# A decoder step with experts: router products on h, grouped routing steps and norm sums on VectorE

## The reference, cut to what matters

```python
h = h + mixer_block(rmsnorm(h, g_mix), ...)        # convolution heads and SSD heads
h = h + hier_moe(rmsnorm(h, g_ffn), ...)
h = h + (p @ w_ple) * sigmoid(rmsnorm(h, g_ple) @ w_ple_gate)
y = rmsnorm(h, g_final)
# rmsnorm(x, g) = x * rsqrt(mean(x * x) + 1e-6) * g
# hier_moe, per row t: softmax over 4 groups, take the best group;
#   of its 4 experts take the best two; out = sum of weight * expert(t)
#   expert(t) = (silu(t @ w_gate_e) * (t @ w_up_e)) @ w_down_e
```

## Time and profile before

| what | value |
|---|---|
| median of three runs | 634.99 us (632.8 to 636.8) |
| the profiled execution | 639.18 us, its span 637.5 us |
| busy: TensorE, VectorE, ScalarE, GpSimd | 584.7, 265.0, 165.3, 81.3 us |
| the chain that ended last | TensorE 71%, DMA 14%, VectorE 5%, ScalarE 4% |
| out projection, second half, ends | 313.9 us |
| expert loop | 349 to 587 us |
| granted TensorE clock, mean | 0.955 of 2.4 GHz |

### The profile page before, as it was taken

How to read it: one execution, slowest core, us unless ns; L and a number is a source line. 1 busy time by engine, 2 the same in 40 slices (tenths; PEclk the granted TensorE clock), 3 DMA queues, 4 the chain that set the end, 5 groups by cost and what they waited for, 6 DMA issues and landing times.

```text
span 637.5 us, 8072 instructions
## 1 busy us (share of the span) xinstructions
PE 584.7 (92%) x2961; PEld 384.5 (60%) x2961; DVE 265.0 (42%) x797; ACT 165.3 (26%) x376; POOL 81.3 (13%) x90
## 2 busy tenths in 40 slices
PE   4999999999889987999877999999999999999993
PEld 3688888868677775888645343434343434434782
DVE  1699888503384786101155023224040404132333
ACT  3211311142457686321213010101101110103313
POOL 4000056023124430020000000000000000000000
PEclk9899999999779998999978989899999999998998
DMA  9643344378415542277941799999999999997001
GB/s 338 197 156 133 137 162 165 114 50 230 156 67 148 190 135 91 76 265 301 422 189 59 282 401 416 420 417 425 421 421 421 424 421 421 422 421 325 0 1 68
DMA packets 30171, 157.86 MB, mean 248 GB/s; under 512 B 6168, under 2 KB 8520, under 8 KB 13760
## 3 DMA queue, kind: packets, MB, share of 16 engines
q1 hardware_dynamic: 24960, 139.69, 55.8%
q0 software_dynamic: 4864, 17.54, 9.2%
q10 hardware_dynamic: 320, 0.27, 0.1%
HBM read 147.13 MB, written 8.21 MB: 244 GB/s over the span
## 4 chain that ended last, share of the span: by engine, by line
PE 71%; DMA 14%; DVE 5%; ACT 4%; issue 2%; SPq 1%; POOLq 0%; DVEq 0%; ACTq 0%
PE ps L796 18%; DMA xbc<-u_rows,slot_tok 11%; PE ps L1059 9%; PE ps L931 9%; PE ps L1030 9%; PE ps L1085 5%; PE ps L1073 4%; PE ps L763 2%; PE ps L846 2%; DMA ring<-glu 2%; PE ps L989 2%; PE ps L787 2%; SPq L347 1%; PE ps L983 1%; PE ps L811 1%
## 5 line engine op out<-in xcount | busy, mean ns | idle before, releaser
L796 PE MATMUL ps<-u,ring 128*128 128x264 f32 x640 | 144.1, 387 | 0.0
L796 PEld LDWEIGHTS ps<-u,ring 128*128 128x128 f32 x640 | 121.0, 190 | 21.1 <-issue 0.4
L1030 PE MATMUL ps<-ring,xraw 128*64 128x512 f32 x512 | 114.7, 601 | 1.2 <-ACT xraw L714 1.2
L1030 PEld LDWEIGHTS ps<-ring,xraw 128*64 128x64 f32 x512 | 35.7, 138 | 68.9 <-issue 68.8
L1503 DVE TENSOR_TENSOR h<-h,ps 128x264 f32<-128x264 f32 x64 | 27.5, 429 | 87.6 <-PE ps L1073 86.7
L931 PE MATMUL ps<-cat,ring 128*128 128x264 f32 x256 | 59.9, 394 | 2.8 <-DVE cat L1352 2.8
L1059 PE MATMUL ps<-ring,xraw 128*64 128x512 f32 x256 | 59.7, 620 | 0.0
L931 PEld LDWEIGHTS ps<-cat,ring 128*128 128x128 f32 x256 | 49.7, 195 | 12.0 <-issue 3.2
L507 POOL DMA_INDIRECT xbc<-u_rows,slot_tok x9 | 8.5, 948 | 285.6 <-DVE slot_tok L1469 285.6
L1059 PEld LDWEIGHTS ps<-ring,xraw 128*64 128x64 f32 x256 | 18.3, 144 | 36.2 <-issue 36.2
L464 POOL TENSOR_TENSOR glu<-asg 128x256 f32<-128x256 f32 x8 | 21.4, 2670 | 99.4 <-ACT asg L578 99.4
(11 more groups left out here) (252 smaller groups left out, 664.8 us busy)
## 6 DMA issues: line engine op xcount, KB each, us to landing
ring<-in_w_moe SPq DMA_DIRECT2D x96, 1024.0 KB, 14.0
ring<-in_w_in SPq DMA_DIRECT2D x20, 1024.0 KB, 5.0
ring<-in_w_out SPq DMA_DIRECT2D x8, 1024.0 KB, 4.9
ring<-in_state_s POOLq DMA_DIRECT2D x8, 512.0 KB, 9.5
out_h_s_out<-ring POOLq DMA_DIRECT2D x8, 512.0 KB, 5.6
ring<-in_w_pleg SPq DMA_DIRECT2D x4, 1024.0 KB, 20.0
ring<-glu SPq DMA_DIRECT2D x48, 32.9 KB, 2.6
h<-in_xT SPq DMA_DIRECT2D x2, 528.0 KB, 4.7
```

The source lines that it names most:

```text
L796: ins = mm(ps[:, BANK[n], 0:T], wv[:, k, q * P:(q + 1) * P], u[:, k, :], start=(k == 0), stop=(k == KD - 1))
L1030: ins = mm(ps[e * CAP:(e + 1) * CAP, gu, :], xg[:, 4 * hf + k, e * CAP:(e + 1) * CAP], wv[:, k, :], start=(hf == 0 and k == 0), stop=(hf = ...
```

## The change

- `load_table(Ln)` loads a table set that holds Ln and Exp, in place of a call of Ln.
- Norm 2: u is h x gain without the root, made by ScalarE behind each square. VectorE adds up the squares of seven blocks; TensorE adds the last and takes the mean (`mean_of_sum`).
- The router's weights are multiplied by the gain on GpSimd, and its products run on h itself: four blocks at a time, each into its own 32 partitions of a PSUM bank (`raw_logits`). VectorE multiplies the result by the root; a product with `fold` adds the four groups and turns to token order. Biases are added there.
- Token rows get the root when ScalarE copies them out (`keep_rows`), which needs the root in token order (`rs_tok`).
- Group and experts are chosen in one pass over five sets of four (the groups and each group's experts). The slots' base is a product with `iota16`; places and totals are two separate waits. The weights of the rows are worked out behind the slot list.
- The p product is split: blocks 0 and 1 ahead of the place products, 2 and 3 ahead of the slot products, 4 to 7 behind.
- Gate: ScalarE makes u as h is added; VectorE squares and adds up for norm 3. Norm 4: VectorE adds up squares between blocks, ScalarE makes `yo` = h x gain, and VectorE multiplies by the root two blocks at a time.
- `fold` gets a tile of its own, and three loads at the start share a semaphore.

```diff
             def load_table(func):
+                if func == ACT.Ln:
+                    a.preload_act_table_set("natural_log_exp_and_others")
+                    return
                 a.activation(warm[:, n_warm[0]:n_warm[0] + 1], eps[:, 0:1], func)
...
                 square(2, c, sq2)
-            root(2)
+                a.activation(u[:, c, :], h[:, c, :], ACT.Copy, scale=par("g_ffn", c)).then_inc(u_ready, 1)
+            root(2, rs_ffn)
+            act.wait_ge(logt_psum, 2)
+            a.activation(rs_tok[:, 0:2], ps[:, 0, 300:302], ACT.Copy)
+            link(a.activation(rs_tok[0:NSM, 2:3], ps[0:NSM, 0, 302:303], ACT.Copy))
+            def keep_rows(t):
+                tn = TOK[t][1]
+                act.wait_ge(utok_psum, t + 1)
+                a.activation(utok[0:tn, t, :].rearrange("p (b n) -> p b n", b=2), ps[0:tn, 2 + 2 * t:4 + 2 * t, :],
+                             ACT.Copy, scale=rs_tok[0:tn, t:t + 1]).then_inc(utok_ready, 1)
+            keep_rows(0)
+            keep_rows(1)
...
-                square(3, c, cat)
+                a.activation(u[:, c, :], h[:, c, :], ACT.Copy, scale=par("g_ple", c)).then_inc(u_ready, 1)
...
+            def mean_of_sum(i, x, last, between=None):
+                bank = NORM_BANK[i]
+                pe.wait_ge(sq_sum, i - 1)
+                ins = mm(ps[:, bank, 0:T], mean_k[:, :], x[:, 0, :], start=True, stop=not last)
+                if between:
+                    between()
+                for c in last:
+                    pe.wait_ge(sq_ready, KD * (i - 1) + c + 1 - (KD if i == 4 else 0))
+                    ins = mm(ps[:, bank, 0:T], mean_k[:, :], x[:, c, :], start=False, stop=(c == last[-1]))
+                ins.then_inc(stat_ready, 1)
...
-            for n in range(KD + 2):
-                if n < KD:
-                    w_out_half(n, 1).then_inc(o_psum, 1)
-                if n >= 2:
-                    mean_square(2, sq2, n - 2)
...
+            def raw_logits(half):
+                pe.wait_ge(o_added, 4 * half + 4)
+                for b in range(4):
+                    c = 4 * half + b
+                    ins = mm(ps[32 * b:32 * b + 32, 1, 0:T], wr[:, c, :], h[:, c, :], start=(half == 0), stop=(half == 1))
+                return ins
+            for n in range(KD):
+                w_out_half(n, 1).then_inc(o_psum, 1)
+                if n == 5:
+                    pe.wait_ge(wr_ready, 1)
+                    raw_logits(0)
+            mean_of_sum(2, sq2, [KD - 1], lambda: raw_logits(1).then_inc(log_psum, 1))
...
+            pe.wait_ge(utok_ready, 2)
+            ple_rows(0)
+            ple_rows(1)
             pe.wait_ge(assigned, 1)
...
-                if j == 0:
-                    for c in range(KD):
-                        mean_square(3, cat, c)
-                if j >= 3:
-                    mean_square(4, cat, j - 3)
+                if j == 1:
+                    mean_of_sum(3, cat, [])
+            mean_of_sum(4, cat, [KD - 2, KD - 1])
...
-            dve.wait_ge(o_added, KD)
-            normed(u, "g_ffn", 2, u_ready)
+            link(v.tensor_copy(raw, ps[:, 1, 0:T]))
+            dve.wait_ge(rs_ready, 2)
+            v.tensor_tensor(logit_f, raw, rs_ffn, ALU.mult).then_inc(logf_ready, 1)
...
+            first_of(sets, top1, d1, c1, low1, oh1)
+            link(v.scalar_tensor_tensor(out=d2, in0=oh1, scalar=-1e30, in1=sets, op0=ALU.mult, op1=ALU.add))
+            first_of(d2, top2, d2, c2, low2, oh2)
...
-            for k in range(KD):
-                v.tensor_scalar(u[:, k, :], h[:, k, :], par("g_ple", k), None, ALU.mult).then_inc(u_ready, 1)
+            link(v.tensor_tensor(cat[:, 0:8, :], h[:, :, :], h[:, :, :], ALU.mult))
+            link(v.tensor_tensor(cat[:, 0:4, :], cat[:, 0:4, :], cat[:, 4:8, :], ALU.add))
+            link(v.tensor_tensor(cat[:, 0:2, :], cat[:, 0:2, :], cat[:, 2:4, :], ALU.add))
+            v.tensor_tensor(cat[:, 0, :], cat[:, 0, :], cat[:, 1, :], ALU.add).then_inc(sq_sum, 1)
...
-            normed(yo, "g_final", 4, yo_ready)
+            rs = ps[:, NORM_BANK[4], 0:T].unsqueeze(1).to_broadcast([P, 2, T])
+            for j in range(0, KD, 2):
+                v.tensor_tensor(yo[:, j:j + 2, :], yo[:, j:j + 2, :], rs, ALU.mult).then_inc(yo_ready, 2)
```

More of the change, by code:

```diff
@@ L12 @@
 from contextlib import ExitStack
+import math
 import numpy as np
@@ L101, in build @@
         warm = sb("warm", [P, 12])
+        fold = sb("fold", [P, 32])
         glu = sb("glu", [P, KD, KC - 1 + NPR])
@@ L198, in build @@
         in_x = [sem(f"in_x{i}") for i in range(2)]
-        in_prm, in_h, in_dt, in_cs, in_ss, in_wr, in_p = [sem("in_" + n) for n in
-            ("prm", "hparams", "wdt", "conf_s", "ssm_s", "router", "ple")]
+        in_small, in_cs, in_ss, in_wr, in_p = [sem("in_" + n) for n in
+            ("params", "conf_s", "ssm_s", "router", "ple")]
         in_st = [sem(f"in_state{i}") for i in range(STATES)]
@@ L308, in build @@
         yo_ready = sem("yo_ready")
+        sq_sum = sem("sq_sum")
+        gained = sem("gained")
         block = ctx.enter_context(nc.Block())
@@ L744, in _ @@
                     square(4, j - 1, cat)
+                    a.activation(yo[:, j - 1, :], h[:, j - 1, :], ACT.Copy, scale=par("g_final", j - 1))\
+                        .then_inc(gained, 1)
             act.wait_ge(h_ple, KD)
             square(4, KD - 1, cat)
+            a.activation(yo[:, KD - 1, :], h[:, KD - 1, :], ACT.Copy, scale=par("g_final", KD - 1)).then_inc(gained, 1)
             root(4)
@@ new lines, in _, with turn_tokens @@
+            for n in range(KD):
[4 more added lines that the diff above has]
+            mean_of_sum(2, sq2, [KD - 1], lambda: raw_logits(1).then_inc(log_psum, 1))
+            def turn_tokens(t):
+                t0, tn = TOK[t]
+                for j in range(KD):
+                    pe.wait_ge(u_ready, KD + j + 1)
+                    ins = tr(ps[0:tn, 2 + 2 * t + j // 4, (j % 4) * P:(j % 4 + 1) * P], u[:, j, t0:t0 + tn], ident[:, :])
+                ins.then_inc(utok_psum, 1)
@@ L965, in _, with ple_rows @@
-                for j in range(KD):
-                    ins = tr(ps[0:tn, 2 * t + j // 4, (j % 4) * P:(j % 4 + 1) * P], u[:, j, t0:t0 + tn], ident[:, :])
-                ins.then_inc(utok_psum, 1)
+                ins = mm(ps[0:tn, 0, 300 + t:301 + t], rs_ffn[:, t0:t0 + tn], ident[:, 0:1], start=True, stop=True)
+            ins.then_inc(logt_psum, 1)
+            turn_tokens(2)
+            def ple_rows(j):
+                if j >= 2:
+                    pe.wait_ge(pw_ready, j - 1)
+                for k in range(2):
+                    ins = mm(ps[:, 3 + j % 2, 0:T], w_ple_k[k][:, j * P:(j + 1) * P], pt[:, k, :], start=(k == 0),
+                             stop=(k == 1))
+                ins.then_inc(pw_psum, 1)
@@ L973, in _ @@
                     vn = TOK[v][1]
-                    ins = mm(ps[0:tn, 6, 16 * t:16 * t + 16], (before if v == t else ones)[0:vn, 0:tn],
+                    ins = mm(ps[0:tn, 1, 384 + 16 * t:400 + 16 * t], (before if v == t else ones)[0:vn, 0:tn],
                              a12[0:vn, v, :], start=(v == 0), stop=(v == t))
+            ins.then_inc(pos_psum, 1)
+            pe.wait_ge(utok_ready, 1)
             for v, (_, vn) in enumerate(TOK):
-                ins = mm(ps[:, 6, 48:64], ones[0:vn, :], a12[0:vn, v, :], start=(v == 0), stop=(v == 2))
+                ins = mm(ps[:, 0, 304:320], ones[0:vn, :], a12[0:vn, v, :], start=(v == 0), stop=(v == 2))
             ins.then_inc(pos_psum, 1)
@@ L990, in turn_rows @@
                 ins.then_inc(xg_psum, 1)
-            pe.wait_ge(in_p, 16 * 3)
-            pe.wait_ge(assigned, 1)
-            pe.wait_ge(utok_ready, 1)
-            for j in range(KD):
-                if j == KD // 2:
-                    pe.wait_ge(utok_last, 1)
-                    pe.wait_ge(sel_ready, 1)
-                    slot_tokens()
-                if j >= 2:
-                    pe.wait_ge(pw_ready, j - 1)
-                for k in range(2):
-                    ins = mm(ps[:, 7 * (j % 2), 0:T], w_ple_k[k][:, j * P:(j + 1) * P], pt[:, k, :], start=(k == 0),
-                             stop=(k == 1))
-                ins.then_inc(pw_psum, 1)
+            ple_rows(2)
+            ple_rows(3)
+            pe.wait_ge(utok_ready, 3)
+            pe.wait_ge(sel_ready, 1)
+            slot_tokens()
+            for j in range(4, KD):
+                ple_rows(j)
             pe.wait_ge(tok_ready, 1)
@@ L1521, in _ @@
                 v.tensor_tensor(h[:, j, :], h[:, j, :], sg[:, j % 4, :], ALU.add).then_inc(h_ple, 1)
+                if j >= 3:
+                    ins = add_square(4, cat, j - 2)
+                    if j == KD - 1:
+                        ins.then_inc(sq_sum, 1)
+                    else:
+                        link(ins)
                 if j + 1 < KD:
```

225 lines of the change are left out of this document (119 added, 106 removed).

## The result

The changed kernel takes 616.01 us (median of 4 runs, 612.6 to 618.85) against 635.89 (632.8 to 638.82) for the kernel before on the same chip: a ratio of 0.9684, interval 0.965 to 0.9717. The forecast was 613.4 with a range of 609 to 619. The gain is 20 us; the profiled pair shows 23.4 (639.18 and 615.78), because the profiled execution of before took longer than each of its four other runs.

What follows compares the result with a forecast made beforehand. TensorE's chain was taken as the bound (71% of the span), with a fixed-length expert loop; savings of 1.28 + 1.28 + 1.7 + 9.8 + 7.5 = 21.6 us from the 634.99 median gave 613.4 us, range 609 to 619.

Steps and rivals of the forecast that it cites:

- First norm: In the first norm's root, the table load between Ln and Exp goes and 1.28 us is passed on.
- Gated norms: In the mixer, the table load between four logarithms and four roots leaves the chain: 1.28 us.
- the three front terms: Savings ahead of the routing: first norm 1.28, gated norms 1.28, second half of the out projection 1.7 us.
- Out projection, second half: Mean products leave TensorE (2.2 us), the first router half comes (0.55): net gain 1.7, range 0.4 to 1.7.
- were they not abreast: Router half in the out projection: eight products not run beside each other would take 1.8 us, not 0.55.
- Routing: Last column to slot list cast: 9.8 us earlier, assuming p products 0 and 1 at half clock; 11.9 at full, 8.3 at worst.
- The store of the token rows: Before the first gather: store ends at 324.6, cast at 326.9, so the store is hidden by 2.3 us.
- The rival: Routing stays at full clock and the token-row store ends last: term 11.9 instead of 9.8, total 611.3; chance 0.2.
- only if the routing gained about 12: Condition before the first gather: the token-row store would end last only with a routing gain of about 12 us.
- The end: Behind the loop: 5.5 us to the last gate product, 1.3 to the final scaling, 0.7 there; 7.5, range 6.0 to 8.0.
- The loop: Expert loop: a block of fixed length, its instructions unchanged, its gathers still 29.1 us apart.
- The last rival: Expert loop: down products and scatter at half clock after the gather's wait, up to 10.8 us a step; near 645; chance 0.02.

Runs made afterwards that it cites:

- x1: The changed kernel run and profiled again without any edit: 611.6 us, ratio 0.9679 to the kernel before.
- x3: The changed kernel with calls of Ln in place of the one table set, so the loads return: 619.11 us, ratio 0.984.
- x4: The kernel before with the table set alone added: 624.46 us over three executions, ratio 0.9872.
- x11: x6 with p products 0 and 1 moved behind the totals, 2 and 3 behind the slot products: 610.08 us, ratio 0.9661.
- x2: The changed kernel with the token-row stores issued by ScalarE behind its last copy, instead of by SP: 615.05 us.
- x6: The changed kernel with the token-row stores ahead of the last two prefetch tiles in SP's queue: 611.7 us, ratio 0.9659.
- x10: The changed kernel with the router's eight products in turn into one group of 32 partitions, not abreast: 613.7 us, ratio 0.9699.
- x9: x6 plus fewer unread filler matmuls in TensorE's waits than x8 had: 602.81 us, ratio 0.9553 to the kernel before.
- x8: x6 plus the first, larger set of unread filler matmuls ahead of six TensorE waits: 610.75 us.
- x5: The kernel before run and profiled again without any edit: 635.89 us.
- x7: The changed kernel plus the first, larger set of unread filler matmuls ahead of six TensorE waits: 612.26 us.

## Why the prediction was right, and where its terms were off

The time (616.0, and 611.6 in x1) fell into the range and close to the forecast of 613.4. In the profiled pair the sum was 21.6 and the measure 23.4. The gain comes in the places that were forecast, but that the terms add up so well is partly luck: the front gave more than forecast, the end less, and the routing came out right by two errors.

- **First norm: 1.28 forecast, 3.85 measured.** The load is 1.28, as x3 shows by itself. The rest, 2.6, is the clock of the step products (2.90, less the later start): half in both profiles of before, full in all eleven profiles without the load. x3, with the load and full clock, shows that the load's wait does not always bring half clock. I had priced the wait and not what runs behind it.
- **Gated norms: 1.28 forecast, 1.29 by x3 and x4.** Behind it is again a clock term that I had left out: the first 48 passes of the out projection take 12.6 us in before, 13.9 in x3 and 10.9 in after. It cannot be credited to the load alone: of the seven profiles with the short wait (1.57 in place of 2.85) and no fillers, x4 and x11 take 12.6 as well. Part of these clock gains is lost again inside the mixer, where after has half clock in other places. At the end of the out projection the lead is 7.2 to 8.2, where the three front terms had promised 4.3; and x2, x6 and x11, with the same instructions up to there, have 9.1, 7.2 and 11.4 (counted from the first profile of before). So what is above the 4.3 varies by execution and cannot be credited to the change alone.
- **Out projection, second half: 1.7 forecast, 1.4 measured** (the lead grows from 5.80 at 256 us to 7.24 at its end), with the router halves at 0.58 and 0.66 for the 0.55 of the working. x10 shows the "were they not abreast": 1.97 each, where 1.8 was worked out.
- **Routing: 9.8 forecast with half clock, 11.9 with full.** Up to the assignment the working held: logits in token order 3.67 behind the last addition to h for 3.65, the choice 3.99 for 4.25. To the cast it was 12.5 at full clock (after, x1) and 10.8 at half (x2): both ends existed, 0.6 and 1.0 above their estimates. Which of them comes is not in the instructions; "half clock" was the step that I took as likeliest, and the first two profiles showed the other. Full clock (2.7 more than the 9.8) less the wait for the store (2.1) makes a net of 10.4: near the forecast by luck.
- **The store of the token rows.** The rival had said: if the clock stays full, the store ends last. That happened. Its condition ("only if the routing gained about 12") was met at 12.5; the store was on its forecast time, by the luck told above, and cost the gather 2.1 us in after and 2.8 in x1, which the rival's 11.9 had not taken off. Of what the gather gained, 17.65 for a forecast of 14.1, the front gave 3.0 of the surplus and the routing 0.6.
- **The end: 7.5 forecast, 6.0 and 7.1 measured.** The gate's 4.9 is exact. Half clock in the last six passes costs 1.05 in some executions (after, x6 and x10; not x1, x2, x3 and x11, all behind 2.36 us of waiting). Of the rest, the way from the table load behind the loop to the first gate product gave 0.35 for the 0.6 of u, the piece to the final scaling 1.1 at full clock for 1.3, and the scaling 0.75 for 0.7; the table's 1.28 was 1.37.
- **The loop: forecast as unchanged.** Its instructions are, but it takes 241.8 to 247.0 in four profiles, because single steps take 2 us more. The last rival read from one pair of gathers, 29.13 apart, that half clock behind the gather does not happen in before; it does, in steps of 31.49 and 31.01 at the loop's start. The 29.1 was right for most steps, and the rival's half clock in every step did not come. The spread of single steps is a good part of the spread of the runs, and it is why a forecast of the sum alone can be right to some 3 us and no better.

What was not tried: whether the start of before would run at full clock in a larger number of profiles (two were half, x3 with the same wait was full), and the undoing of VectorE's sums of squares, or of the grouped choice, by itself: those parts are read from rows only.

## What to carry to other kernels

A term that shortens a wait of TensorE can have a second part, the clock of the matmuls behind the wait. At the first norm it was twice the first (2.9 and 1.29), but it differs from execution to execution, so give it as a range. Work put into the waits (sized to fit: the first set overran them and gained nothing) brought 7 to 9 us more than the stores ahead alone (by the ratios and by the medians of x9 and x6). When a stage is shortened by 12 us, list every transfer that it hid and give each its end and its tail; here the next one late cost 2 to 3 us of it. And when two profiles of the same instructions differ, compare stage by stage before you explain a total.

## What was not expected of the hardware

- After one and the same wait, 1.58 us ahead of the p products, the granted clock was 1.00 in after and x1 and 0.50 in x2, x8 and x9; after 2.96 us at the start it was 1.00 in x3 and, after 2.95, 0.50 in x5. TensorE's wait alone does not decide it.
- The DMA queues did not end together. Behind full queues (1.0, 426 GB/s) a share of 0.07 stayed busy for 2 us, with the store on SP's queue (after) and on ScalarE's (x2), and the gather, which waits for the whole store, paid for that.
- Products of 32 columns beside each other take 0.66 us for eight passes, one behind the other 1.97.
- One filler, a product of 128 columns, makes two records and takes 0.245 us (26 records in 3.17 us in x7), 0.12 a pass; a pass of 264 columns takes 0.22.
